# A hybrid block with four token mixers on one core: shared value projections, attention scores on both row halves, local-attention probabilities one step ahead, and a later merge

## The reference, cut to what matters

```python
x = concatenate([112 zero pads, 16 meta tokens, x])        # 640 slots; 512 are real
h = rms_norm(x)
z = h @ W_in            # aq ak av | bq bk bv bg | c_in | dq dk dv | four gates of 1024
y_sb  = stick_breaking_attention(aq, ak, av)                # 8 heads of 64, all earlier keys
y_ret = silu(bg) * retention(bq, bk, bv)                    # 4 heads, keys 64, values 128
y_rw  = rwkv7_mix(rwkv7_project(c_in, ...))                 # 8 heads of 64, chunked
y_sw  = sliding_window_attention(dq, dk, dv)                # 8 q heads, 2 kv heads, window 128
merged = sum_i sigmoid(gate_i) * (y_i @ P_i)
x = x + merged @ W_o
x = x + relu(rms_norm(x) @ W_up)**2 @ W_down
```

## Time and profile before

| | |
|---|---|
| median of 3 runs | 1241.03 us (1238.74 to 1241.16) |
| the profiled execution | 1239.84 us, of which the span of the instructions is 1238.1 us |
| PE busy | 1193.8 us, 96% of the span |
| DVE, ACT, POOL busy | 501.7, 494.0, 466.1 us |
| mean granted clock of PE | 0.995 of full speed |
| the chain that ended last | PE 77%, DVE 11%, ACT 6% |
| DMA | 110.18 MB, 89 GB/s over the span |

### The profile page before, as it was taken

How to read it: one execution, slowest core, us unless ns; L and a number is a source line. 1 busy time by engine, 2 the same in 40 slices (tenths; PEclk the granted TensorE clock), 3 DMA queues, 4 the chain that set the end, 5 groups by cost and what they waited for, 6 DMA issues and landing times.

```text
span 1238.1 us, 21307 instructions
## 1 busy us (share of the span) xinstructions
PE 1193.8 (96%) x9094; PEld 986.6 (80%) x9094; DVE 501.7 (41%) x1001; ACT 494.0 (40%) x815; POOL 466.1 (38%) x288
## 2 busy tenths in 40 slices
PE   8999999999999999999999999889899999999998
PEld 7998877977898587676677777679888888888886
DVE  4799335444444643442443765361522100222000
ACT  6455223232323435666636525332634311333220
POOL 3352544334433143323322523144244544344541
PEclk9999999999999999999999999999999999999999
DMA  6222323122301131112412311242133332222330
GB/s 243 86 86 77 121 87 118 62 83 79 112 29 53 51 137 53 35 35 91 185 52 77 105 40 64 77 145 69 49 107 101 119 101 87 85 93 94 119 119 34
DMA packets 33344, 110.18 MB, mean 89 GB/s; under 512 B 4050, under 2 KB 6066, under 8 KB 32611
## 3 DMA queue, kind: packets, MB, share of 16 engines
q1 hardware_dynamic: 25952, 92.44, 22.4%
q10 hardware_dynamic: 6786, 16.26, 3.5%
q0 software_dynamic: 512, 0.13, 0.1%
HBM read 99.43 MB, written 9.04 MB: 88 GB/s over the span
## 4 chain that ended last, share of the span: by engine, by line
PE 77%; DVE 11%; ACT 6%; issue 2%; POOL 2%; DMA 1%; ACTq 0%; DVEq 0%
PE pst L1720 17%; PE pst L1722 16%; PE pst L1721 16%; PE pst L1903 5%; PE pst L1902 5%; PE pst L1901 5%; ACT w_hi L843 2%; PE pst L2212 1%; POOL w_lo L725 1%; DMA sw_v<-wait_sw_v 1%; PE pst L2204 1%; PE pst L1940 1%; PE pst L1927 1%; PE pst L1993 1%; PE pst L2174 1%
## 5 line engine op out<-in xcount | busy, mean ns | idle before, releaser
L725 POOL TENSOR_TENSOR w_lo<-raw,w_hi 128x1024 fp32r<-128x1024 f32 x164 | 399.8, 2443 | 657.2 <-ACT w_hi L843 645.5
L1720 PE MATMUL pst<-h_hi,w_hi 128*128 128x512 f32 (+1 forms) x704 | 256.1, 364 | 1.5 <-DVE h_lo L1288 0.7
L1722 PE MATMUL pst<-h_hi,w_lo 128*128 128x512 f32 (+1 forms) x704 | 243.0, 345 | 0.0
L1721 PE MATMUL pst<-h_lo,w_hi 128*128 128x512 f32 (+1 forms) x704 | 242.7, 345 | 0.0
L843 ACT ACTIVATE w_hi<-raw 128x1024 fp32r<-128x1024 f32 x164 | 171.3, 1051 | 149.0 <-PE pst L1903 114.2
L1720 PEld LDWEIGHTS pst<-h_hi,w_hi 128*128 128x128 f32 x704 | 133.3, 189 | 25.9 <-issue 5.6
L1722 PEld LDWEIGHTS pst<-h_hi,w_lo 128*128 128x128 f32 x704 | 133.0, 189 | 16.0
L1721 PEld LDWEIGHTS pst<-h_lo,w_hi 128*128 128x128 f32 x704 | 133.4, 190 | 15.1 <-issue 2.2
L1720 PE MATMUL pst<-x_hi,w_hi 128*128 128x512 f32 (+1 forms) x272 | 103.3, 380 | 3.8 <-POOL w_lo L725 2.0
L1722 PE MATMUL pst<-x_hi,w_lo 128*128 128x512 f32 (+1 forms) x272 | 103.2, 379 | 0.0
L1721 PE MATMUL pst<-x_lo,w_hi 128*128 128x512 f32 (+1 forms) x272 | 103.1, 379 | 0.0
(11 more groups left out here) (336 smaller groups left out, 2150.5 us busy)
## 6 DMA issues: line engine op xcount, KB each, us to landing
raw<-in_weights SPq DMA_DIRECT2D x164, 512.0 KB, 3.4
xt<-in_x SPq DMA_DIRECT2D x4, 512.0 KB, 5.4
wait_gate<-stage ACTq DMA_DIRECT2D x8, 256.0 KB, 2.0
gate_t<-wait_gate ACTq DMA_DIRECT2D x1, 2048.0 KB, 8.4
x<-in_x ACTq DMA_DIRECT2D x1, 2048.0 KB, 8.7
out<-x SPq DMA_DIRECT2D x8, 256.0 KB, 3.3
cst<-in_consts SPq DMA_DIRECT2D x1, 1524.0 KB, 11.2
wait_ret_v<-stage ACTq DMA_DIRECT2D x8, 128.0 KB, 1.9
```

What stands on the lines that cost most here:

```text
L725: nc.gpsimd.tensor_tensor(w_lo[:, u % W_SLOTS, :], raw[:, u % RAW_SLOTS, :], w_hi[:, u % W_SLOTS, :].bitcast(F32), ALU.subtract).then_inc( ...
L1720: M(out, lh, rh, start=(first and i == 0), stop=False)
L1721: M(out, lh, rl, start=False, stop=False)
L1722: last = M(out, ll, rh, start=False, stop=(final and i == len(terms) - 1))
```

## The change

1. *Values.* The second pair of retention's value heads and the local attention's values become one job of 384 columns from three units (`bdv`, five jobs of 24 matmuls in three pieces). The jobs before the RWKV blocks come in another order, and five pieces fewer stand ahead of the first level of a block (RW_FILL, 4 becomes 3, five times).
2. *lora.* Its four matmuls are issued alternately from the lower and the upper rows.
3. *Scores.* Copies of q and k with the row halves exchanged (sb_qx, sb_kx) are made by DMAs from SBUF to SBUF, four for each pair of heads, on SP's queue among the weight loads. From head 1 on, key blocks 1 and 3 are scored from the copies, in the other half of the rows. Key block 3 moves from bank 6 to the end of bank 5, so that blocks 1 to 3 are 768 columns in one piece.
4. *Reload.* The spilled projections are reloaded on SP's queue in ten DMAs, ahead of the weight unit 65, when the last stick-breaking output is summed (o_done 4), not on ACT's queue when its low half is written.
5. *Tanh and retention gate.* The tanh of the first four gates goes from head 7 to `ret_gate`, where the same two table loads serve it and retention's gate. The multiplication on DVE goes behind `ret_out(0)`. PE waits for values at b = 1 and for y_lo at b = 2.
6. *Local attention.* `sw_probs(i + 1)` is issued behind `sw_turn(i)`, `sw_probs(0)` ahead of `sw_scores(1)`. `sw_turn(i)` on PE also waits until DVE has read the scores i + 1 (ds_read). 24 pieces as before, (1, 2) eight times.
7. *Merge.* `merge_tile` comes one job later, the table load leaves `load_x2`, and jobs 0 and 1 of W_o do their k = 0 to 6 first, both, and then k = 7 of both.

Some semaphores are merged (tanh_done, keys_copied, par_ready).

```diff
-RW_FILL = [dict(tok=1, score=0, c1=[4, 1, 1, 1, 1], tu=[0, 1, 1, 2, 2], f=1, wz=1, mn=1, end=2)] + \
+RW_FILL = [dict(tok=1, score=0, c1=[3, 1, 1, 1, 1], tu=[0, 1, 1, 2, 2], f=1, wz=1, mn=1, end=2)] + \
...
-SW_FILL = [(2, 2)] * 2 + [(2, 1)] * 4 + [(1, 1)] * 2
+SW_FILL = [(1, 2)] * 2 * NB
...
-          [("rgate", BRANCH_RW, i) for i in range(KD)] + av_jobs("bv") + \
-          [("bg", t, 0) for t in range(4)] + \
-          [("dq", t, 0) for t in range(4)] + [("dk", 0, 0)] + [("dv", 0, b) for b in range(NB + 1)] + \
+          [("rgate", BRANCH_RW, i) for i in range(KD)] + \
+          [("bv", 0, b) for b in range(NB + 1)] + [("bg", 0, 0)] + \
+          [("bdv", 0, b) for b in range(NB + 1)] + \
+          [("bg", t, 0) for t in range(1, 4)] + \
+          [("dq", t, 0) for t in range(4)] + [("dk", 0, 0)] + \
...
-            g("reload_late")
             g("ret_prep")
...
                 g("sw_square", b)
+                if b == 0:
+                    g("ret_gate_low")
...
             g("sw_scores", 0)
+            g("sw_probs", 0)
             for i in range(2 * NB):
                 if i + 1 < 2 * NB:
                     g("sw_scores", i + 1)
-                g("sw_probs", i)
                 pieces(SW_FILL[i][0])
                 g("sw_turn", i)
+                if i + 1 < 2 * NB:
+                    g("sw_probs", i + 1)
                 pieces(SW_FILL[i][1])
                 g("sw_out", i)
...
             for k in range(KD):
                 jobs(1)
-                g("merge_tile", k)
-            jobs(len(PHASE_O) - NB)
+                if k:
+                    g("merge_tile", k - 1)
+            g("merge_tile", KD - 1)
+            jobs(len(PHASE_O) - NB - 1)
+            g("norm2_tables")
+            jobs(1)
...
+            def swap_halves(t):
+
+                for to, at_ in ((slice(0, HD), slice(HD, P)), (slice(HD, P), slice(0, HD))):
+                    sp.dma_start(sb_kx[t % 2][to, :].rearrange("p (a b) -> p a b", a=2),
+                                 sb_k[at_, t, MB:].rearrange("p (a b) -> p a b", a=2)[:, :, P:2 * P])\
+                        .then_inc(swap_in[t % 2], 16)
+                    sp.dma_start(sb_qx[to, t % 2, :], sb_q[at_, t, P:T]).then_inc(swap_in[t % 2], 16)
...
+                sp.wait_ge(o_done, 4)
...
+                if u == UNIT_NO[("p", BRANCH_SB, 1)]:
+                    reload_late()
                 weight_unit(u)
...
-                    if b % 4 == 3:
+                    if b % 4 == 3 and (a, b) != (BRANCH_SB, 3):
...
             def ret_gate():
                 use_tables("exp_and_others")
+                act.wait_ge(job_out["gate"], 4)
+                A(gate_t[:, 0:4], gate_t[:, 0:4], ACT.Tanh, scale=0.5).then_inc(gate_tanh, 1)
...
+                    us = u % W_SLOTS
+                    nu = len(units_of(JOBS[n]))
+                    o = pst[0:r, 2 * s, 0:P * nu].rearrange("p (a f) -> p a f", a=nu)
+                    wsl = lambda w, k: w[:, us:us + nu, P * k:P * k + P]
...
+                    if a == 0 and b < 2:
+                        for k in range(KD - 1):
+                            if b == 0:
+                                pe.wait_ge(m_lo, k + 1)
+                            wo_part(n, b, k)
+                        if b == 1:
+                            pe.wait_ge(m_lo, KD)
+                            wo_part(n - 1, 0, KD - 1).then_inc(dense_done, 1)
+                            wo_part(n, 1, KD - 1).then_inc(dense_done, 1)
...
-            SB_AT = [(4, 0), (5, 0), (6, 0), (6, 2 * P)]
+            SB_AT = [(4, 0), (5, 0), (6, 0), (5, 3 * P)]
...
+                    if h and kb in (1, 3):
+                        keys = sb_kx[t % 2][other, P * (kb // 2):P * (kb // 2) + P]
+                        queries = sb_qx[other, t % 2, P * (kb - 1):T - P]
+                    else:
+                        keys, queries = sb_k[r, t, MB + P * kb:MB + P * kb + P], sb_q[r, t, P * kb:T]
...
                 pe.wait_ge(dp_ready, i + 1)
+                if i + 1 < 2 * NB:
+                    pe.wait_ge(ds_read, i + 2)
```

More of the change, by code:

```diff
@@ L112, in units_of @@
         return [("w_in", base + 2 * a), ("w_in", base + 2 * a + 1)]
+    if kind == "bdv":
+        return [("w_in", BV + 2), ("w_in", BV + 3), ("w_in", DV)]
     if kind in ("gate", "rgate"):
@@ L142, with converted_after @@
 assert all(UNIT_NO[units_of(j)[0]] % 2 == 0 for j in JOBS if j[0] in ("av", "bv", "wo"))
+assert UNIT_NO[("w_in", BV + 2)] % W_SLOTS + 3 <= W_SLOTS
+def converted_after(n):
+    us = units_of(JOBS[n])
+    more = {"bv": 2, "bdv": 1}.get(JOBS[n][0], 0) if n == LAST_JOB[UNIT_NO[us[0]]] else 0
+    return UNIT_NO[us[0]] + W_SLOTS + more
 def pack_weights(w_in, p_sb, p_ret, p_rw, p_sw, w_o, w_up, w_down):
@@ L326, in build @@
         sb_end_at = at[0]
+        at = [SBUF_BASE + 4 * CONST_AT["rw_mask"][0]]
+        sb_qx = place("sb_qx", [P, 2, T - P], at=at)
+        sb_kx = [place("sb_kx0", [P, 2 * P], at=at), place("sb_kx1", [P, 2 * P], at=[top + 4 * (SB_N - T)])]
+        assert at[0] <= SBUF_BASE + 4 * CONST_AT["suffix"][0] and SB_N - T + 2 * P <= 2 * T
         sb_s_hi = [place("sb_s_hi0", [P, T], F32R, at=lor_at), place("sb_s_hi1", [P, SB_N - T], F32R, at=[top])]
@@ L398, in build @@
         const_in, table_in = sem("const_in"), sem("table_in")
+        swap_in = [sem(f"swap_in{i}") for i in range(2)]
         xb_in = [sem(f"xb_in{b}") for b in range(NB)]
@@ L780, in pieces @@
                     if part == parts - 1:
[L781 removed]
+                        low(converted_after(n))
                     piece[0] += 1
@@ L1794, in lora @@
                 for i in range(2):
-                    last = M(pst[:, 4 + i, 0:HL], w2[:, P * t:P * t + P], WA[0:HD, HL * i:HL * i + HL],
-                             start=True, stop=True)
-                last.then_inc(lora_done, 1)
-                for i in range(2):
-                    last = M(pst[:, 6 + i, 0:HL], a2[:, P * t:P * t + P], WA[HD:P, HL * i:HL * i + HL],
-                             start=True, stop=True)
-                last.then_inc(lora_done, 1)
+                    w_last = M(pst[:, 4 + i, 0:HL], w2[:, P * t:P * t + P], WA[0:HD, HL * i:HL * i + HL],
+                               start=True, stop=True)
+                    a_last = M(pst[:, 6 + i, 0:HL], a2[:, P * t:P * t + P], WA[HD:P, HL * i:HL * i + HL],
+                               start=True, stop=True)
+                w_last.then_inc(lora_done, 1)
+                a_last.then_inc(lora_done, 1)
             def kksum(t):
@@ L1870, in job @@
                                         k == 0, k == KD - 1)
-                    last.then_inc(dense_done, 1)
+                    if a == 0 and b < 2:
[8 more added lines that the diff above has]
+                    else:
+                        for k in range(KD):
+                            last = wo_part(n, b, k)
+                        last.then_inc(dense_done, 1)
                 elif kind == "up":
```

164 lines of the change are left out of this document (88 added, 76 removed).

## The result

The changed kernel takes 1226.84 us (median of 4 runs, 1225.2 to 1227.15) against 1241.1 before (4 runs, 1238.74 to 1241.36): a ratio of 0.9887, 95% interval 0.9869 to 0.9904, or -14.3 us. The forecast was 1224.3 in a range of 1216 to 1232.5. The profiled executions are 1239.84 before and 1227.15 after, -12.7, and it is this difference that the traces can explain.

A forecast was written before the change was run, and what follows sets the result against it. PE bounds the kernel, busy 1193.8 of 1238.1 us. Terms -4.8 - 1.8 - 1.8 + 0 - 2.5 + 0 - 4.7 = -15.6 from 1239.84 give 1224.2; forecast 1224.3, 8-in-10 range 1216 to 1232.5.

The forecast's parts named there:

- the likeliest case: Whole kernel: the forecast itself, 1224.3 us, own range 1219.5 to 1229; chance 0.52.
- Values: Value projections: 120 matmuls of 384 columns, 0.18 us each, replace 26.4 us by 21.6: -4.8, ends -6 and -2.5.
- signs named for being wrong: PE standing over 5 us in retention, or bdv's first matmul waiting for w_lo, would show the forecast wrong.
- lora: lora matmuls: different row halves already run side by side, so 0; by the program-order rule 2.2 us would be gained.
- Scores: Stick-breaking scores on both row halves: 0.6 us saved in each of heads 2, 4, 6: -1.8, ends 0 and -4.2.
- the slack of heads 2, 4 and 6: Stick-breaking: DVE ends the low half at 501.11, PE reads it at 503.16, so these heads gain 0.6 each.
- Tanh: Head 7 of stick-breaking: the tanh and two table loads leave ACT, PE's wait for masked weights goes: -1.8.
- Reload: Retention: PE waits less for ret_vm, more for squares behind unit 65: 0, ends -2.5 and +2.5.
- Local attention: Five waits for probabilities go, -6.1, a first wait of +3.6 comes: net -2.5, ends -6.1 and 0.
- The new fall of the clock: Local attention: a fall of 1.7 us behind the first wait replaces the one at 776: 0.
- Merge: Merge and W_o: waits of 2.1 and 1.3 and one clock fall of 1.7 go, 0.4 returns: -4.7, ends -5.7 and -1.5.
- The slower rival: SP's queue: unit 65 lands behind the reload at 614 or beyond, PE lacks pieces: 1240 and more; chance 0.07.

The follow-up runs named there:

- the undoing: Changed kernel with one edit put back: the tanh in head 7, 1229.21 us; or, for local attention, the old order of the probabilities and fill table, 1229.25 us.
- the second profile: Profile of the changed kernel run again without any edit, beside the other variants of its set: 1226.84 us, ratio 0.9894.
- the two improvements together: Changed kernel with weight unit 65 ahead of the reload, gates ahead of values, and earlier fill in local attention: 1215.35 us, ratio 0.9796.

## Why the prediction was right, step by step

The direction, the range and the likeliest case held. The sum of -15.6 was 2.9 too good against the profiled execution. Its terms were off on both sides by up to 1.7, and that they nearly cancel is luck.

- *Values: -4.8 forecast, -6.5 measured up to stick-breaking.* The distance of 0.18 for 384 columns was nearly right (0.17 to 0.18). With the medians of the whole traces, 0.175 for 384 columns and 0.119 for 256, the same working gives -5.3. The rest is PE's waits inside the RWKV blocks, which I had not counted at all: those for ACT's rw_c and rw_wz were 2.5 and are 0.7, and others grew by some 0.5. The fill that was taken away in the first levels did leave its cover just whole, as said: PE comes at 180.49, POOL's masks end at 180.33 (compare):

```profile
177.90 2.43 POOL L864 TENSOR_TENSOR rw_m<-rw_scores,cst 128x256 f32<-128x256 f32 x3 [0.45 <-DVE rw_scores L1663]
...
180.49 0.69 PE L2279 MATMUL pst<-rw_t,rw_m 64*64 64x64 f32 x32
```

  One of the signs named for being wrong did come: bdv's first matmul waits for w_lo. It is 0.18 us once, and it refutes nothing but the way the sign was put, without a size.
- *lora: 0 forecast, 0 measured.* The upper rows start ahead of the second lower matmul in the order of before (47.59 against 48.14), so there was no 2.2 to gain.
- *Scores: -1.8 forecast, -0.8 to -1.2 measured.* The saving inside a head was right (0.6), and so was that only every other head shows it. What failed is the slack of heads 2, 4 and 6: PE ran into POOL's mask of the head before, 0.2, 0.2 and 0.7.
- *Tanh: -1.8 forecast; -2.0 by the trace, -2.4 by the undoing.*
- *Reload: 0 forecast, +1.6 measured.* The mechanism was named: less for ret_vm, more for the squares, behind unit 65. Its size was not: I had the new wait take the place of the old ones and left out the clock. The wait of 2.8 for the squares did take the place of waits of 1.6, 0.9 and 0.4 us, and 1.7 of clock came on top (3.4 in the second profile). The 1.6 is the whole stage's: the moved tanh, the moved multiplication and the split values are in it, and the reload by itself was not undone.
- *Local attention: -2.5 forecast, -1.7 by the trace, -2.4 by the undoing.* The new first wait was forecast as 3.6 later in the program, and by the same points (695.31 before, 688.60 after, a lead of 6.7 less the moved piece of 2.8, against 7.2) it is 3.3:

```profile
688.11 0.34 DVE L1593 TENSOR_TENSOR sw_scores<-pst,cst 128x64 f32<-128x64 f32 x2
...
688.60 1.09 PE L2178 MATMUL pst<-cst,sw_scores 128*128 128x128 f32 x4 [3.13 <-DVE sw_scores L1593]
```

  DVE ends the read and PE starts, as the order of instructions said (compare). The five waits for probabilities all went, also those where I feared that DVE had no slack. What the sum left out is the wait of 1.8 for y_lo that came within the last scores. The new fall of the clock came too: 3.3 in the first profile and 1.7, as priced, in the second.
- *Merge: -4.7 forecast, -3.8 measured, -5.3 in the second profile*, which has no fall of the clock there at all. The waits and the fall at 812 went. The reason that I gave for the 2.1, the split one job behind, is only one of two: taking away the table load was enough too.

The slower rival, the weights behind the reload on SP's queue, was the right place to look: unit 65 did come late by 1.36 on ACT. But ACT begins its conversion at 589.92, ahead of the 598 that I expected and far from the 614 at which the sum would be lost.

## What to carry to other kernels

Put a bulk reload behind the next small transfer that an in-order engine needs, not ahead of it. Here 0.5 MB ahead of 4.7 MB, together with the gates ahead of the values, was worth 4.4 us, part of it clock. When a chain is moved one step ahead, its first step has no predecessor to hide in. Give that step its own fill: here two pieces took away 6.2 us of waits and brought 1.6 back elsewhere. Look at where new waits stand before you name their cause: that 1.6 was not where the fill had been taken. And undo each of two edits that aim at one wait by itself, and both together: here either was enough, and neither undoing alone shows the other's worth.

## What the runs showed of the hardware

The clock does not fall with every wait of one length. The changed kernel and the one with earlier fill in local attention run the same program up to there, and both stand about 3 us in the window of 588 to 592 (2.8 and 3.5). In the changed kernel, with PE busy for 1.20 of 4 us, the clock fell to 0.57 in the 4 us behind it (shown above):

```profile
588.00:592.00 4.00, 1.20 (x6) 0.68 (x5) 1.42 (x1) 2.16 (x3) 0.95 (x1) 1.00 0.85 346
```

In the other it stayed whole, though PE stood longer:

```profile
588.00:592.00 4.00, 0.50 (x3) 0.15 (x2) 1.39 (x1) 2.50 (x4) 0.67 (x1) 1.00 0.82 333
592.00:596.00 4.00, 4.00 (x23) 3.13 (x24) 1.49 (x4) 1.34 (x3) 1.68 (x1) 1.00 0.32 102
```

Two profiles of the changed kernel put their falls at different places (592, 688, 880; and about 588, 688, 764) with nearly the same waits. What is a cost of 1.7 us in one execution is none in another, so a prediction should carry the clock as a chance per wait and not as a term of the sum.

Small steps of DVE took several times their length beside POOL's conversions of weights: 1.68 for 0.16 (4 elements a partition) and 2.20 for 0.29 (128 elements) in the run with earlier fill, and 1.66 and 2.20 in the two improvements together. That POOL is the reason is argued from the coincidence in time. A sum of terms that are each read from a quiet place does not see it.

Matmuls from different halves of the rows overlap: in lora in both orders of the program (0.80 us a turn in either), and in the scores, issued in turn (1.74 for 2.35).
